# Differential attention woven into the mixer's projections and output product, by pairs of heads

## What is computed

```
q_x, k_x, v_x, gu_x, gv_x = split(hx @ w_in)          # x tokens
k_c, v_c = split(hc @ w_in[:, k and v columns])       # context tokens
k_all, v_all = concat([k_c, k_x]), concat([v_c, v_x]) # 512 keys, 8 heads
s = einsum('bqhmd,bkhmd->bhmqk', q, k_all) / 8        # m = 2 score maps a head
p = softmax(s);  a = p[:, :, 0] - lam * p[:, :, 1]
o = einsum('bhqk,bkhe->bqhe', a, v_all)
a_x = o * rsqrt(mean(o * o) + 1e-5) * norm_g * 0.8    # per head
g_x = gelu(gu_x) * (w_s @ layer_norm(gelu(gv_x)) + b_s)   # four groups
y = concat([a_x, g_x]) @ w_out
```

## Time and profile before

| | us |
|---|---|
| time, median of 3 runs (lowest, highest) | 2215.3 (2212.99, 2216.16) |
| the profiled execution's own time | 2214.42 |
| its span in the trace | 2212.6 |
| PE busy / DVE busy / ACT busy in it | 1827.7 / 1467.5 / 882.3 |
| the change's stage in it, from x ready to `rn` | 404.6 to 720.4 |
| from `rn` to the first experts' fetch | 720.4 to 747.0 |

### The profile page before, as it was taken

How to read it: one execution, slowest core, us unless ns; L and a number is a source line. 1 busy time by engine, 2 the same in 40 slices (tenths; PEclk the granted TensorE clock), 3 DMA queues, 4 the chain that set the end, 5 groups by cost and what they waited for, 6 DMA issues and landing times.

```text
span 2212.6 us, 21909 instructions
## 1 busy us (share of the span) xinstructions
PE 1827.7 (83%) x7101; PEld 1097.5 (50%) x7101; DVE 1467.5 (66%) x3019; ACT 882.3 (40%) x2302; POOL 620.3 (28%) x567
## 2 busy tenths in 40 slices
PE   4888999899868687988877877996889888877786
PEld 3757998799656444434322333354434343322222
DVE  6767956955675666677567777525576777677755
ACT  3446433522443234344434444312343444444433
POOL 1160000000000334434354443203244344444441
PEclk9889989998988799999999999997999999999999
DMA  9754757646344599999999999845899999999995
GB/s 369 264 197 146 267 186 296 238 183 248 105 143 145 209 384 416 421 418 421 380 418 422 421 422 421 343 171 218 360 418 420 419 421 421 421 421 421 421 422 247
DMA packets 114690, 723.76 MB, mean 327 GB/s; under 512 B 11504, under 2 KB 13344, under 8 KB 34064
## 3 DMA queue, kind: packets, MB, share of 16 engines
q0 software_dynamic: 74864, 540.30, 59.0%
q1 hardware_dynamic: 39712, 182.07, 22.1%
HBM read 721.24 MB, written 1.08 MB: 326 GB/s over the span
## 4 chain that ended last, share of the span: by engine, by line
PE 40%; DMA 30%; DVE 19%; issue 5%; ACT 5%; POOL 1%; SPq 0%; DVEq 0%; ACTq 0%; POOLq 0%
DMA X<-in_k_uv,EI 15%; PE PS L2020 14%; DMA Z<-in_k_uv,EI 8%; DMA W<-in_peer_wq 5%; PE PS L1997 5%; PE PS L1709 5%; PE PS L1710 4%; PE PS L1711 4%; DVE junk L1696 4%; DVE ACC L1320 3%; DVE WL L1336 2%; PE PS L1797 2%; DMA W<-in_ada_w 2%; PE PS L2073 1%; PE PS L2035 1%
## 5 line engine op out<-in xcount | busy, mean ns | idle before, releaser
L2020 PE MATMUL PS<-X,dg 128*128 128x512 f32 x1372 | 669.1, 623 | 166.6 <-ACT dg L908 160.1
L1696 DVE CUSTOM_DVE_ANT_0 junk<-H,X 128x1024 f32<-128x1024 f32 x343 | 420.0, 1224 | 239.3 <-DMA X<-in_k_uv,EI 229.2
L899 POOL DMA_INDIRECT X<-in_k_uv,EI x343 | 377.8, 1101 | 618.8 <-PE PS L2020 375.7
L2020 PEld LDWEIGHTS PS<-X,dg 128*128 128x128 f32 x1372 | 249.0, 194 | 543.0 <-ACT dg L908 328.0
L908 ACT ACTIVATE CF<-DOT 128x1 f32<-128x1 f32 x512 | 102.2, 200 | 576.8 <-DVE DOT L1696 567.2
L2020 PE MATMUL PS<-Z,dg 128*128 128x512 f32 x504 | 248.0, 625 | 53.0 <-ACT dg L908 52.7
L908 ACT ACTIVATE dg<-CP,CG 128x128 f32<-128x128 f32 x512 | 205.7, 402 | 17.5 <-PE PS L2020 0.7
L1696 DVE CUSTOM_DVE_ANT_0 junk<-H,Z 128x1024 f32<-128x1024 f32 x126 | 154.2, 1224 | 85.7 <-DMA Z<-in_k_uv,EI 76.6
L2020 PEld LDWEIGHTS PS<-Z,dg 128*128 128x128 f32 x504 | 92.0, 195 | 191.0 <-ACT dg L908 115.9
L899 POOL DMA_INDIRECT Z<-in_k_uv,EI x126 | 137.3, 1089 | 142.4 <-PE PS L2020 122.0
L1709 PE MATMUL PS<-XH,WH 128*128 128x256 f32 x592 | 173.6, 293 | 2.4 <-ACT XH L908 1.2
(11 more groups left out here) (298 smaller groups left out, 2642.5 us busy)
## 6 DMA issues: line engine op xcount, KB each, us to landing
W<-in_ada_w SPq DMA_DIRECT2D x50, 1024.0 KB, 6.5
Y<-in_ada_w SPq DMA_DIRECT2D x22, 1024.0 KB, 5.5
W<-in_peer_wq SPq DMA_DIRECT2D x16, 1024.0 KB, 16.2
W<-in_k_ffi SPq DMA_DIRECT2D x13, 1024.0 KB, 6.6
Y<-in_k_ffi SPq DMA_DIRECT2D x9, 1024.0 KB, 5.1
W<-in_ffn_w_out SPq DMA_DIRECT2D x8, 1024.0 KB, 5.4
W<-in_k_win SPq DMA_DIRECT2D x8, 1024.0 KB, 6.1
Y<-in_k_win SPq DMA_DIRECT2D x8, 1024.0 KB, 7.5
```

Source lines behind the costliest of these rows:

```text
L899: e.indirect_dma_start(out=WS[k][:, :], out_offset=None, in_=I[f"k_uv{ly}"][:, :], in_offset=bass.IndirectOffsetOnAxis(ap=EI[t][:, j:j + 1 ...
L1696: e.tensor_tensor_reduce(junk, H[:, t, :], d[:, 0:D], 1.0, 0.0, ALU.mult, ALU.add, DOT[:, j:j + 1]).then_inc(v_dot, 1)
L2020: p = e.matmul(PS[:, 2 * t + q, :], dgb[n % 4][:, :], d[:, D + q * 512:D + (q + 1) * 512], start=(j == 0), stop=(j == 127))
```

## The change

The stage from `xt(2)` to `rn` is ordered anew. The work is the same but for the norm over heads, and the steps are now these:

- The projection parts go by pairs of heads (`WIN_ORDER`: q, k, v of heads 0 and 1 of four each, and so on; g and u tiles last), and units by head, so that a unit needs only its own pair's tiles.
- After 20 quarters (with the context's transposes between) comes a loop over units n and five places k. Each place takes one piece of attention and then one quarter from `fillers()`, which gives the 76 quarters of projections that are left and then the output parts. Of unit n, `ds` stands at place 1, the maximum (`dm`) at 2, the exponentials (`de`) at 3, `dn` at 4; `dt` follows at place 2 of the next unit, `do` at place 0 of the one after. So three units are in flight.
- `ada` steps are at place 4 of each unit and at place 0 of each odd one. Weight loads stand at a part's end, right ahead of their split. `ring3` stands ahead of `xt(2)`: three slots for the whole stage, since the exponentials' buffers now lie where `Y0` and `Y1` were.
- The norm goes by four units: each output is copied from PSUM to `OB` (ACT) with its square sum (ACT), scaled on DVE (`hs`, `hs2`), and transposed two heads later (`turn_head`).
- Output parts go in the order 0, 1, 2, 4, 5, 3 (`AO_ORDER`). Rows 3 and 4, `fold` and `sc` are in the last steps ahead of the last six quarters; row 5 is in the experts' stage, and the last `modp` behind the output product.

```
-WIN_ORDER = list(range(8)) + [14, 15, 12, 13] + list(range(8, 12))
+WIN_ORDER = [0, 4, 8, 1, 5, 9, 2, 6, 10, 3, 7, 11, 14, 15, 12, 13]
+AO_ORDER = [0, 1, 2, 4, 5, 3]
...
+    P("ring3")
...
+    for n in range(18):
+        for k in range(5):
+            if k == 0:
+                if n - 2 in units:
+                    P("do", n - 2)
+            elif k == 1:
+                if n in units:
+                    P("ds", n)
+                if n - 2 in units:
+                    P("dc", n - 2)
+            elif k == 2:
+                if n - 1 in units:
+                    P("dt", n - 1)
+                if n in units:
+                    P("dm", n)
+                if n > 4 and n % 4 == 1:
+                    P("hs", n // 4 - 1)
+            elif k == 3:
+                if n - 1 in units:
+                    P("da", n - 1)
+                if n in units:
+                    P("de", n)
...
+            else:
+                if n in units:
+                    P("dn", n)
+                if n > 4 and n % 4 == 1:
+                    P("hs2", n // 4 - 1)
+            if k == 4 or k == 0 and n % 2:
+                step(5 if n < 15 else 2)
...
+            next(g)
...
+    row(4, 1, 0)
+    next(g)
+    row(4, 2, 1)
+    next(g)
     P("fold", 0)
     P("sc", 0)
...
+    for _ in g:
+        pass
+    for _ in part(5):
+        pass
+    P("modp", 9, 0)
...
-        order = [(t, hd) for t in range(2) for hd in range(8)]
+        order = [(t, hd) for hd in range(8) for t in range(2)]
...
-                        w.wait_ge(p_row, 12)
+                        w.wait_ge(p_do, 16)
+                        w.wait_ge(p_row, 10)
```

More of the change, by code:

```diff
@@ L195, in make_plan @@
     P("post", 1, 1)
+    P("ring3")
+    P("ldctx")
+    P("ldlam")
     for c in range(8):
-        xt(2, c, bank(low))
-    P("ldctx")
-    P("lam")
+        xt(2, c, 4 + c % 4)
     split(IN + 1)
[L201 to L253, removed]
@@ L254, in make_plan, with products @@
-    P("gn8")
-    for c in range(8):
-        xt(4, c, bank(low))
+    def products():
+        group, rope, pend = 0, 0, None
+        for i in range(16):
+            n, tile = IN + i, WIN_ORDER[i]
+            for q in range(quarters(n)):
+                b = 6 + group % 2
+                P("gq", n, q, b)
+                if q in (2, 5) and pend is not None:
+                    P("rope2", *pend)
+                    pend = None
+                if q == 3:
+                    P("evac", n, b, rope)
+                    if tile < 8:
+                        pend = (rope, tile)
+                        rope += 1
+                    group += 1
+                elif q == 7:
+                    P("evc", n, b)
+                    group += 1
+                if q == quarters(n) - 1:
+                    P("ldw", n + 2)
+                    split(n + 2)
+                yield
@@ new lines, in make_plan, with step, turn_head, part @@
+    steps = iter(range(43, 72))
+    mods = {47: 6, 55: 7, 63: 8}
+    due = []
+    def step(b):
+        while due:
+            mod(due.pop(), b)
+        m = next(steps, None)
+        if m is not None:
+            ada(m)
+            if m in mods:
+                due.append(mods[m])
+    def turn_head(h, b):
+        P("xp", 4, h, b)
+        P("xt", 4, h, b)
+        P("xl", 4, h)
+    def part(i):
+        n = AO + i
+        for q in range(4):
+            P("gq", n, q)
+            yield
+            if q == 3 and i < 4:
+                P("ldw", n + 2)
+                split(n + 2)
@@ L257, in make_plan @@
+    turn_head(6, 2)
+    next(g)
+    turn_head(7, 3)
+    P("rowv", 4)
+    next(g)
+    row(4, 1, 0)
+    next(g)
+    row(4, 2, 1)
+    next(g)
     P("fold", 0)
     P("sc", 0)
[L259 to L269, removed]
+    for _ in g:
+        pass
+    for _ in part(5):
+        pass
@@ L1770, in xin @@
             def xin(i, t):
-                return both(XH, XL)(i, t) if i < 8 else both(GSH, GSL)(i - 8, t)
+                if i < 8:
+                    turned(4, i)
+                    return chunk(XTS[4][1], i, t), chunk(XTS[4][2], i, t)
+                w.wait_ge(a_xth, nth.use["gate", i - 8])
+                w.wait_ge(v_xtl, nth.use["gate", i - 8])
+                return chunk(GSH, i - 8, t), chunk(GSL, i - 8, t)
             for kind, *a in plan:
```

324 lines of the change are left out of this document (196 added, 128 removed), and 2 rows, old and new, of tables (d_gath, p_x).

## The result

| | us |
|---|---|
| before, median of 4 runs (lowest, highest) | 2214.96 (2212.99, 2216.16) |
| changed, median of 4 runs (lowest, highest) | 2198.04 (2196.49, 2200.78) |
| ratio, 95% interval | 0.9926 (0.9909 to 0.9943) |
| profiled execution of the changed kernel, and its span | 2196.84, 2195.0 |

What follows compares the result with a forecast made beforehand. PE was taken to bound the stage: 404.6 + 253.8 of PE work and dips + 8 for DVE + 3.0 for fold put rn at 669.4 instead of 720.4, 51.0 us less. Forecast 2164 us, range 2145 to 2192.

Steps and rivals of the forecast that it cites:

- PE's pace and start-up: Stage on PE: projection quarter 1.44 us, output quarter 1.36, unit 2.55; start-up to the first product 7 us.
- Small matmuls: Stage on PE: 64 transposes for context and heads, 48 row matmuls, 16 of gates, at 0.12: 15.4 us.
- What DVE takes back: Units: DVE keeps up on average but exceeds PE in some; 8 us charged, bounds 0 and 19.
- three dips of 1.75: PE's clock falls to its lower level behind each of three modps, 1.75 us each, 5.2 in all.
- DVE's waits sum to more than 50 us: Sign named in advance that the prediction is wrong, read in the changed profile.
- for which PE waits up to 3.5: Stage: modp 6 follows its last ada by one place, so PE waits up to 3.5 us.
- PE starved in clusters: Rival, 0.19: DVE, ACT and PE wait in turn, the clock falls; one to three more stops, 2174 to 2194.
- All hidden: Rival, 0.15: PE never waits for DVE and dips are short; 2151, down to 2143.
- The ring: Rival, 0.05: three load slots are too short for the stage; slower than before, 2235 at 1.5 us per load.
- The end: Before rn: R1 lands after 5.5 us, fold 3.7, sc 0.6; rn waits 3.0 us for fold.
- Row 5 ... nothing: Experts' stage: row 5's few PE and ACT operations among fetches cost nothing; 2 us without that cover.
- passed on whole: Behind rn: fetches pace the kernel, so whatever the stage gains reaches the end whole.

Runs made afterwards that it cites:

- e11: Head 4 turned in PSUM bank 4, not the product with v's, against a kernel joining row 5 in one go, later modp 6, later gn 1, earlier ada (0.9838): 0.9858.
- e4: Changed kernel with DVE multiplying 8 columns instead of 2048 from ada 48 on, all loads kept (work left out): ratio 0.9864.
- e2: Changed kernel with modp 6 three places later, ada 48 and 49 moved too: ratio 0.9876.
- e10: As e4, but the loads from ada 48 on bring only 8 columns too (work left out): ratio 0.9868.
- e1: Changed kernel with row 5 formed in one go in the experts' stage instead of in five steps: ratio 0.9891.
- e15: On e2, the second token tile's first route moved ahead of cols and the rows, row 5 still in five steps: ratio 0.9823, median 2175.94 us.
- e13: Changed kernel with both the 8 columns of e4 and the copies of e5 (work left out): ratio 0.9852.
- e5: Changed kernel with Gelu of g and u tiles and Sqrt of gn 1 and the heads' norm made plain copies (work left out): ratio 0.9888.
- e14: Changed kernel with the edits of e1 and e2 together, nothing else: ratio 0.9837.
- e8: On e2, modp 6, 7 and 8 form only one of their 16 columns (work left out): ratio 0.9815.
- e9: On e2, modp 6 to 8 cut into four pieces of four columns between quarters, with ada steps moved: ratio 0.9927.
- e17: On e15, modp 6 to 8 in four pieces, those of modp 7 and 8 a place later than in e9: ratio 0.9852.

## Why the prediction was wrong, step by step

- *PE's pace and start-up*: right. 9.77 us a unit with its quarters; the first score maps at 446.6 against 445.5 by the prices. That products would not slow down beside attention was right.
- *Small matmuls*: "64 transposes for context and heads" was a miscount. The trace has 16 and 16, so PE's work was 3.8 us less than the sum said: 649.4 for the input of `rn` at the prices, without dips.
- *What DVE takes back, 8 us (bounds 0 and 19)*: **this step failed.** The input of `rn` was ready at about 693.0 (row 4's last product ends at 686.1, and five quarters of 1.36 follow), 43.6 behind 649.4, where the sum had 8 and three dips of 1.75, 13.2 in all. By the score maps it was lost so: 1.1 at the start, 11.0 in the unit of `modp 6`, 3.5 and 4.0 at `modp 7` and `modp 8`, 5.0 elsewhere, 19.0 behind unit 15's score maps.
- How it was lost: PE stands 27.4 us in the stage, 12.8 of them in the closing part. So at least 16 of the 43.6 are not stops, and the windows show the clock at its lower level for them, for which the sum had 5.2: 0.50 was granted from 640 to 650, and the units of `modp 7` and `modp 8` lose 3.5 and 4.0 with stops of 1.6 and 0.4, where a dip was priced at 1.75. Of the 5.0 elsewhere 3.1 are in unit 14, where PE stands 2.67 before a product with v, the stop that e11 tested.
- Why it failed: I balanced DVE against PE by units and took what exceeded. Taking 47 us of DVE's work away (e4) gave back 14.5, and DVE was busy only 204.0 of 291.8. What the balance misses is the queues' order: DVE and ACT each stand for one operation of the other that lies behind unrelated work. The waits were forecast in the wrong direction too: DVE waits for exponentials 6.8 us in all, not 20 to 30, and ACT for the maximum 28.5. DVE's longest waits, 36.2 us in all, are for ACT's half of the splits, which my sum did not count (before, they were 42.9); how much of them is on the path was not worked out. My sign "DVE's waits sum to more than 50 us" came, 87.8 us idle, but it could not have told anything: before, DVE was idle 111.5 of 315.8.
- *modp 6, "for which PE waits up to 3.5"*: it stood 6.03, then worked at the low level of its clock for 6.99 and more. e2 shows 8.6 us of the stage for this place alone (7.7 in the units 0 and 1). I had the place and half its price, and counted it under a sum that was then taken at 8. The Trainium skill (TensorE: Matmul & The Clock Gate, "Part 1: The HAM clock gate") has the clock halved behind an idle stretch: the trace agrees here, with 0.53 granted from 460 to 470 after 6.03 idle, and 0.50 from 640 to 650 behind the stop of 5.56. Both stops and what follows them speak for the rival that I gave 0.19.
- *The rivals*: "PE starved in clusters" is what happened, at units 1 and 15/16 as named, and beyond its range (2174 to 2194). "All hidden" is refuted by 43.6 us. The ring is refuted as a cause by the 0.3 us of waits for its loads, and e10 agrees; its 2235 should have been about 2238 by its own terms (2164 + 49 x 1.5). Of ACT's waits for `uT` and table loads no rival spoke.
- *The end*: right, with `fold` read as 3.7 us where the rows give 3.6. `fold` released `rn`, 3.4 us late (3.0 forecast), `R1` landed 5.7 us after its issue, and `rn` to the first fetch took 26.8.
- *"Row 5 ... nothing", and "passed on whole"*: **the second step that failed.** I priced row 5's operations and not its steps. Each step that the plan adds ahead of a route moves the route's date, and the first route of the second tile had no reserve: 6.4 us lost against the kernel before, 10.0 got back by e1, 7.2 by e15 (single traces; e1's ratio gives 8).

Sum of the difference: the stage gave 24.0 where 51.0 was forecast, with 43.6 - 13.2 = 30.4 more lost to stops and the clock, 0.4 more at `fold`, and 3.8 less PE work: 27.0. The other 6.4 were given back behind `rn`. 17.6 us are left in the spans.

What stays open: about 5 us of the closing part, with DVE's load and the tables gone. Five stops of PE stand there in e13, 3.9 us in all, the longest of 2.17 before a turned head's transposes (`OB`); no run took them away. What decides whether the clock falls at a whole `modp` is open too: runs with the same steps differ there by 1.5 to 3 us. e5's gain of 3.6 us ahead of the closing part is in part of this kind: 1.6 of it is at `modp 8`, where e2 and e14 differ by as much with the same steps.

## What to carry to other kernels

Where pieces of several chains are woven in one fixed order on engines that wait in order, balancing busy times by stretch says little: look for each operation that another engine needs soon, and list what stands ahead of it in its own queue and in the queue of whoever feeds it. A consumer one place behind its producer is the first to fail (`modp 6`: 8.6 us for a move of three places). Freed time need not reach the end of the stage: of the 47 us taken from DVE in e4, 14.5 did, and of the 16.2 taken from PE in e8, 11.4. And when a step moves into a list of steps that is consumed at a fixed rate, its cost is the delay of everything behind it, not its own work: ask which of those has no reserve.

## What the hardware showed that I had not expected

- A switch of ACT's tables costs 1.28 us in these rows (639.55, 641.07), and the next operation starts at once. The Trainium skill (ScalarE: Activation LUTs, "What ACT_TABLE_LOAD costs") gives about 2.66 us with a drain; the rows show no such drain, and the rows decide.
- 32 matmuls of one column (a `modp`) take 3.63 us at best. Even when PE does not stand before them, the granted clock can be low in the 10 us around: 0.74 in this window of e2, and 0.66 in e15. It need not be: in e14, with the same steps, the window has 1.00. Cut into four pieces between quarters they take 0.95 to 1.05 each, and the same window has 1.00 too (e9, e17), which by e14 proves nothing for the pieces.

```profile
460.00:470.00 10.00, 10.00 (x63) 9.47 (x63) 7.52 (x12) 2.53 (x6) 0.00 (x0) 0.74 0.53 197
```

```profile
460.00:470.00 10.00, 10.00 (x77) 8.71 (x78) 8.45 (x16) 2.53 (x6) 0.00 (x0) 1.00 0.62 210
```
